# Three products in another order, and low weight slabs at other columns, in a split-fp32 transformer kernel

## The reference

```
proj = h @ w_in                 # 1024 -> 3080 (first), 1024 -> 4608 (second)
mixed @ w_out                   # 1024 -> 1024, and two 512 -> 1024 in the second
silu(conv(a)) * b @ w_down      # a, b = split(h @ w_up); 1024 -> 2*2816 -> 1024
(silu(x @ w_gate) * (x @ w_up)) @ w_down     # four times in the second
```

## The kernel before

| slabs | while high x high streams, the high block again | while low operand streams, the low block | while low weights stream, the next chunk's high block |
|---|---|---|---|
| x, t = 0 or 16 | 16 | 16 | 32 |
| x, t = 14 | 26 | 26 | 42 |
| a, t = 0 or 16 | 16 | 16 | 48 |
| a, t = 14 | 26 | 26 | 58 |
| down, t = 0 or 16 | 16 | 16 | 16 (48 at the change of slab) |
| last down (tokens loaded) | 0 | 0 | 32 |

## Time and profile before

### The profile page before, as it was taken

The page is one execution under the profiler, slowest core; times in us unless marked ns, Lnnn a source line. Parts: engine busy times, 40 slices in busy tenths (PEclk is TensorE's granted clock), DMA queues, the critical chain, the costliest instruction groups (busy, mean ns, idle before and its releaser), DMA issues.

```text
span 1445.7 us, 31241 instructions
## 1 busy us (share of the span) xinstructions
PE 1437.9 (99%) x11649; PEld 1412.6 (98%) x11649; DVE 898.3 (62%) x1568; ACT 770.2 (53%) x1113; POOL 496.2 (34%) x213
## 2 busy tenths in 40 slices
PE   9999999999999999999999999999999999999998
PEld 8899999999999999999999999999999999999987
DVE  6438888745445469989644434444447998864433
ACT  6556565555445446567544544444545567655443
POOL 6550000543334303710244442433420570044442
PEclk9999999999999999999999999999999999999999
DMA  7434566645556545445565654555644545567663
GB/s 268 134 110 160 177 193 190 218 163 163 177 176 213 169 134 164 143 162 161 178 176 176 208 182 134 184 174 187 202 157 140 174 133 180 170 201 205 206 193 111
DMA packets 74779, 250.94 MB, mean 174 GB/s; under 512 B 15824, under 2 KB 16848, under 8 KB 74704
## 3 DMA queue, kind: packets, MB, share of 16 engines
q1 hardware_dynamic: 74416, 249.38, 55.3%
q10 hardware_dynamic: 288, 0.54, 0.1%
HBM read 247.79 MB, written 1.05 MB: 172 GB/s over the span
## 4 chain that ended last, share of the span: by engine, by line
PE 98%; DVE 1%; ACT 1%; issue 0%; DVEq 0%; ACTq 0%
PE W L1784 28%; PE W L1786 28%; PE W L1785 28%; PE XP L1925 2%; PE XQ L1925 2%; PE W L1879 1%; PE W L1841 1%; PE W L1878 1%; PE W L1877 1%; PE W L1843 1%; PE W L1842 1%; PE XQ L2038 0%; PE XP L1930 0%; DVE scr L1429 0%; PE XP L1879 0%
## 5 line engine op out<-in xcount | busy, mean ns | idle before, releaser
L538 POOL TENSOR_TENSOR wlo<-raw,whi 128x1024 fp32r<-128x1024 f32 (+1 forms) x185 | 475.7, 2576 | 899.6 <-ACT whi L618 899.1
L1784 PE MATMUL W<-xh,whi 128*128 128x272 f32 (+2 forms) x2400 | 688.8, 287 | 0.1
L1786 PE MATMUL W<-xh,wlo 128*128 128x272 f32 (+2 forms) x2400 | 685.7, 286 | 0.0
L1785 PE MATMUL W<-xl,whi 128*128 128x272 f32 (+2 forms) x2400 | 679.9, 283 | 0.0
L618 ACT ACTIVATE whi<-raw 128x1024 fp32r<-128x1024 f32 (+1 forms) x440 | 480.9, 1099 | 110.4 <-PE W L1786 71.3
L1784 PEld LDWEIGHTS W<-xh,whi 128*128 128x128 f32 x2400 | 451.6, 188 | 2.5 <-issue 1.5
L1786 PEld LDWEIGHTS W<-xh,wlo 128*128 128x128 f32 x2400 | 453.0, 189 | 0.0
L1785 PEld LDWEIGHTS W<-xl,whi 128*128 128x128 f32 x2400 | 451.7, 188 | 0.2
L1111 DVE TENSOR_TENSOR wlo<-raw,whi 128x1024 fp32r<-128x1024 f32 (+1 forms) x255 | 331.7, 1301 | 80.0 <-ACT whi L618 79.5
L1784 PE MATMUL W<-ax,whi 128*128 128x272 f32 (+2 forms) x992 | 282.9, 285 | 0.6 <-DVE ax L1550 0.4
L1785 PE MATMUL W<-ax,whi 128*128 128x272 f32 (+2 forms) x992 | 282.2, 284 | 0.0
(11 more groups left out here) (287 smaller groups left out, 1216.7 us busy)
## 6 DMA issues: line engine op xcount, KB each, us to landing
raw<-in_w SPq DMA_DIRECT2D x377, 512.0 KB, 3.6
raw<-in_w SPq DMA_DIRECT2D x64, 704.0 KB, 4.0
proj<-proj SPq DMA_DIRECT2D x16, 64.0 KB, 3.9
scr<-in_cst SPq DMA_DIRECT2D x1, 1000.0 KB, 8.0
h<-in_hT SPq DMA_DIRECT2D x3, 272.0 KB, 4.4
raw<-in_w SPq DMA_DIRECT2D x2, 256.0 KB, 3.8
proj<-in_gain SPq DMA_DIRECT2D x1, 512.0 KB, 4.6
out<-proj SPq DMA_DIRECT2D x4, 128.0 KB, 1.8
```

The lines of the kernel that those rows point to most:

```text
L538: pool.tensor_tensor(low(j, place), packed(j, place), high(j, place).bitcast(F32), ALU.subtract).then_inc(lo_ready[j], 1)
L1784: pe.matmul(out, wh, mh, start=start and k == 0, stop=False, skip_group_check=True)
L1785: pe.matmul(out, wh, ml, start=False, stop=False, skip_group_check=True)
L1786: ins = pe.matmul(out, wl, mh, start=False, stop=stop and k == len(pairs) - 1, skip_group_check=True)
```

## The change

The three matmuls of a chunk are put in another order in `slab`, `first_pair`, `first_slab` and `second_slab`: low weights by high operand first, then high by high, then high by low operand. The low slabs of kinds x and a are placed by the chunk before (`t - T`, `t - ROW`), that is, 16 or 32 elements modulo 64 earlier than before. The distance at t = 14 goes from 26 to 18 for both parts. In the last down product the low slab is placed 32 elements later. The numbers of instructions, their shapes, the waits and the DMAs are as before. The distances, once more in the order of the streams:

| slabs | while low weights stream, the high block | while high x high streams, the high block again | while low operand streams, the next chunk's low block |
|---|---|---|---|
| x and a, t = 0 or 16 | 16 | 16 | 16 |
| x and a, t = 14 | 18 | 18 | 18 |
| down | 16 | 16 | 16 (48 at the change of slab) |

In the last down product the order of the matmuls stays, and the third distance goes from 32 to 0.

```diff
-X_BEHIND = {0: -16, T_A: -26, T_B: -16}
-ACT_BEHIND = {0: (-16, -16), T_A: (-26, -26), T_B: (-16, -16)}
+X_BEHIND = {0: -16, T_A: -18, T_B: -16}
+ACT_BEHIND = {0: (-16, -16), T_A: (-18, -18), T_B: (-16, -16)}
 DOWN_BEHIND = {0: (-16, -16), T_B: (-16, -16)}
-TOKEN_BEHIND = (0, 0)
+TOKEN_BEHIND = (0, LINE // 2)
...
-    return Place(DC, P, P + T % LINE, column(X_AT + t, WHI_AT, j, X_BEHIND[t]), column(X_AT + t, WLO_AT, j, X_BEHIND[t]))
+    return Place(DC, P, P + T % LINE, column(X_AT + t, WHI_AT, j, X_BEHIND[t]), column(X_AT + t - T, WLO_AT, j, X_BEHIND[t]))
...
-    return tuple(Place(DC, P, P + ROW % LINE, column(X_AT + t, WHI_AT, j, high), column(X_AT + t, WLO_AT, j, low))
+    return tuple(Place(DC, P, P + ROW % LINE, column(X_AT + t, WHI_AT, j, high), column(X_AT + t - ROW, WLO_AT, j, low))
...
-                    pe.matmul(out, wh, mh, start=start and k == 0, stop=False, skip_group_check=True)
-                    pe.matmul(out, wh, ml, start=False, stop=False, skip_group_check=True)
-                    ins = pe.matmul(out, wl, mh, start=False, stop=stop and k == len(pairs) - 1,
+                    pe.matmul(out, wl, mh, start=start and k == 0, stop=False, skip_group_check=True)
+                    pe.matmul(out, wh, mh, start=False, stop=False, skip_group_check=True)
+                    ins = pe.matmul(out, wh, ml, start=False, stop=stop and k == len(pairs) - 1,
                                     skip_group_check=True)
```

More of the change, by code:

```diff
@@ L1840, in first_pair @@
                         out = W[j][:, t[j]:T]
-                        pe.matmul(out, wh, mh, start=k == 0, stop=False, skip_group_check=True)
-                        pe.matmul(out, wh, ml, start=False, stop=False, skip_group_check=True)
-                        ins = pe.matmul(out, wl, mh, start=False, stop=k == DC - 1, skip_group_check=True)
+                        pe.matmul(out, wl, mh, start=k == 0, stop=False, skip_group_check=True)
+                        pe.matmul(out, wh, mh, start=False, stop=False, skip_group_check=True)
+                        ins = pe.matmul(out, wh, ml, start=False, stop=k == DC - 1, skip_group_check=True)
                         if k == DC - 1:
@@ L1958, in first_slab @@
                     wh, wl = weights(0, first_x(0)[0], k)
-                    pe.matmul(out, wh, xh[:, k, :], start=k == 0, stop=False, skip_group_check=True)
-                    pe.matmul(out, wh, xl[:, k, :], start=False, stop=False, skip_group_check=True)
-                    ins = pe.matmul(out, wl, xh[:, k, :], start=False, stop=k == DC - 1, skip_group_check=True)
+                    pe.matmul(out, wl, xh[:, k, :], start=k == 0, stop=False, skip_group_check=True)
+                    pe.matmul(out, wh, xh[:, k, :], start=False, stop=False, skip_group_check=True)
+                    ins = pe.matmul(out, wh, xl[:, k, :], start=False, stop=k == DC - 1, skip_group_check=True)
                     if k == 2:
@@ L1976, in second_slab @@
                         wh, wl = weights(1, first_x(1)[1], k)
-                        pe.matmul(W[1][:, 0:T], wh, xh[:, k, :], start=k == 0, stop=False, skip_group_check=True)
-                        pe.matmul(W[1][:, 0:T], wh, xl[:, k, :], start=False, stop=False, skip_group_check=True)
-                        ins = pe.matmul(W[1][:, 0:T], wl, xh[:, k, :], start=False, stop=k == DC - 1, skip_group_check=True)
+                        pe.matmul(W[1][:, 0:T], wl, xh[:, k, :], start=k == 0, stop=False, skip_group_check=True)
+                        pe.matmul(W[1][:, 0:T], wh, xh[:, k, :], start=False, stop=False, skip_group_check=True)
+                        ins = pe.matmul(W[1][:, 0:T], wh, xl[:, k, :], start=False, stop=k == DC - 1, skip_group_check=True)
                 ins.then_inc(mm_done, 1)
```

## The result

The changed kernel takes 1450.72 us in the median (1450.42 to 1451.24, 13 runs) for 1447.68 us before (1447.20 to 1448.05, 13 runs): a ratio of 1.002 with a 95% interval from 1.0013 to 1.0028. It became slower by 3.0 us where 7.0 us less was forecast. The two profiled executions, 1447.49 and 1450.50 us, differ by as much.

What follows compares the result with a forecast made beforehand. TensorE, busy 99% of the span, was taken as the bound. Terms of 5.2 + 0.8 - 0.4 + 1.0 + 0.4 = 7.0 us less took 1447.4 to 1440.4 us, range 1425 to 1447.6.

Steps and rivals of the forecast that it cites:

- What bounds the kernel: Whole kernel: TensorE is busy 99% of the span, so only the pitch of the matmuls can give time.
- Kind x with 272 columns: 4752 matmuls in x slabs go from 124.3 to 123.2 ns, the pitch inside a down slab: 5.2 us less.
- The outer bound of this term: x slabs of 272 columns at most fall to 119.7 ns, the fast down slab's per-column rate: 21.9 us less.
- The price as such: At 272 columns the pitch rises with the third distance alone: 16, 32, 48 give 123.2, 124.3, 125.3 ns.
- kind a's 0.8 us: 384 matmuls of 272 columns in a slabs go from 125.3 to 123.2 ns: 0.8 us less.
- Kind x with 256 columns: x slabs of 256 columns, now at 116.9 and 118.3 ns, all come to 117.8 ns: 0.4 us more.
- 258 columns: x and a slabs at distance 18 come to 118.7 ns: 1.0 us less for x, 0.4 us less for a.
- Last down product: Some 200 matmuls of 512 columns, third distance 32 to 0: taken as zero, bound 0.4 us either way.
- `first_pair`, waits and the down slabs: `first_pair` 0.1 us either way, taken as zero; down slabs unchanged, zero; no new waits from low first.
- Rule against row: The skill page's independent TensorE read ports make placement worth 0; the profile rows make it worth 7.0 us.
- The slower rival: Cost hangs on which operand streams while which loads: 2 ns more per chunk, 3.2 us, 1450.6 us; chance 0.12.
- The fast pattern: Equal distances keep the rhythm settled at 113.0 ns: 23.2 us less, 1424.2 us; chance 0.25 including partial cases.

Runs made afterwards that it cites:

- experiment 1: The changed kernel's new matmul order with all placements of the kernel before; ratio 0.9999 to the kernel before.
- experiment 7: Changed kernel with low slabs at t = 0 placed as before: 1443.29 us; second program, adding equal-address 256-column operand chunks in the last MLP up: 1442.78 us.
- experiment 4: Kernel before, x slabs multiplying only chunks 0 and 4 (computation changed); slot 0, both distances 16: 123.3 ns at 272 columns, 113.3 at 256.
- 2: Kernel before, in the old order, with only the low slabs of kinds x and a placed as in the changed kernel; 1452.18 us for 1448.73, ratio 1.0024.
- 5: Kernel before with the chunks of an x slab taken as 0, 4, 1, 5, 2, 6, 3, 7; ratio 1.0002.
- 6: Changed kernel, low slabs at t = 0 as before, kind x's at t = 16 placed 48 from their own operand; 1449.17 us for 1448.69, ratio 1.0004.
- 8: Changed kernel, kind x low slab 8, 4, 12, 24 from its operand by slot; then whole stages, 4 with 12 and 4 with 0: ratios 0.9996 and 1.0011.
- 9: Changed kernel with the low slab of kind x 16 from its own operand at t = 0 and 12 at t = 16; 1441.13 us for 1449.27, ratio 0.9944.
- the first sweep: Changed kernel with the low slab of kind x 0, 16, 32, 48 from its own operand in slots 0 to 3; pitch read by slot, no total time given.

## Why the prediction was wrong

- **What bounds the kernel**: right. TensorE's busy time and the device time rose by the same 3.0 us, and no wait came in.
- **Kind x with 272 columns, 5.2 us less**: this is the step that failed. "All three distances become 16", and "The nearest row is the inside of a down slab, 123.2, for 124.3 now." The stage came out at 126.1 ns, 7.8 us more over all x slabs of 272 columns. The down product has 16 to the stream beside the load and 16 to the load's own operand, because its chunks don't move modulo 64. In x slabs they move by 16, so making the one distance even took the other from 16 to 0. That the new low places at t = 0 cost 7.4 of the 7.8 us is shown by experiments 1 and 7; where both distances are 16, x slabs do have 123.3 ns (experiment 4). Why they cost what they do isn't shown: the same own distance of 0 gave 125.1 ns in the old order (2). The front tables had shown only one of the two distances, and the ordering 123.2, 124.3, 125.3 over three kinds of slab looked like a law of that one. (The outer bound of this term is a little off: 113.0 / 256 x 272 is 120.1 ns and not 119.7. Nothing hangs on it.)
- **The price as such**: a distance has no price that can be added up. 16 at half of the places gave nothing (5), 48 and 4 were among the best in a slot and among the worst in a stage (6, 8). Even kind a's 0.8 us by the same law did not come: 125.3 ns stayed, with its third distance at 16 in place of 48 and, in return, its low blocks 48 from their own operand in place of 16.
- **Kind x with 256 columns, 0.4 us more**: 4.1 us less. The value, 117.8 ns, was off by 2.8 ns; the last mixer and the last MLP up took a pattern of 115.0 ns that no row of before had, and the first model's MLP up 116.6. The remark that this part was weak held, the range of 113.0 to 117.8 for it too.
- **258 columns**: 118.7 ns was forecast. In the first projection it came (118.7, for 120.0, from the starts in the traces), in the first out projection about (118.9), in the MLP up not (119.8 inside a slab, as before). 1.4 us was forecast for both kinds, 0.4 us came.
- **Last down product**: 0.3 us less, inside the bound of 0.4. `first_pair`, waits and the down slabs: about a tenth of a us or less each, as taken.
- **Rule against row**: the page "SBUF — State Buffer" of the Trainium skill, section "Who interferes with whom", gives TensorE independent read ports for operand and weights and says that it never waits on anyone; by that the placement would do nothing. The measurement decides against this for this case: the order alone moves 0.0% (1), the places alone 0.24% (2). Whether the ports are where the time goes, no run shows.
- **The slower rival** named 1450.6 us, and 1450.7 was measured, but for a reason that experiment 1 refutes: with its order and the old places 272 columns stay at 124.2 ns. By line, the longest is now the low-weights line with 292 ns, and the two that should both have 290 have 292 and 287. A number that fits is no proof of its mechanism.
- **The fast pattern**: the forecast for it was 113.0 ns where all distances are equal. With equal chunk addresses this occurs at 256 columns (4), not surely (7), and at 272 columns the level is 123.3.

What stays open: why a sequence settles where it does. The runs show that the pitch moves with the addresses (1, 2), that equal distances modulo 64 elements give the same pitch in all four slots (126.1 ns in each in the changed kernel's MLP up), that it depends on the columns of the stream and on the slabs around (6, 8, 9), and, by the two groups of 7, that it probably differs from execution to execution. No model here foretells the pitch of a sequence that has not been run. Equal chunk addresses at 272 columns with the full computation weren't tried.

## What to carry to other kernels

Where TensorE is the bound and small matmuls follow each other with a new weight block each, read the pitch from starts and counts, stage by stage: 0.5% lay in the columns at which slabs begin. When a row from another stage is taken as the price, list everything in which the two stages differ in the quantity that moves, here both neighbours of a load and not one. And measure a placement over a whole stage: a sweep by slot measures the mixture. In the first sweep the slots at 0 and 16 agreed with their whole stages to 0.3 ns, but of the three slots picked as the best ones, only one kept its pitch. The two sums made of whole stages came out within 0.8 us (7, 9).

## What the runs showed of the hardware

- At the upper clock (granted 0.999) matmuls of 128x128 by 272 float32r columns had 123.4 to 126.1 ns from start to start in whole stages, by placement alone, and those of 256 columns 113.9 to 120.5 ns.
- Which part, high or low, streams or loads made no difference; addresses did (experiment 1, equal in every stage to a few hundredths of a us, the first projection aside).
- The second program of experiment 7 ran in two groups 4.3 us apart, which a median of few runs would hide. The same placement also had two levels inside one program before any change.
- Streams of 512 columns against stationary tokens had 234.1 ns in the earlier trace rows and, with the third distance at 0 in the changed kernel, 29.8 / 43 / 3 = 231.0 ns. Those of 256 columns in the same product went the other way, from 116.6 to 117.8 ns (from the starts), so 0.3 us is what is left of both:

```profile
L1878 PE MATMUL W<-whi,ax x44: 389/392/396, 1383.2 to 1413.0; 128*128 128x512 f32 x44
```
